# First modulation by quarters of columns, with the contraction of 1536 columns begun on each quarter's K-tiles

## The reference, cut to what matters

```
c_act = silu(c)                                    # c: 1 x 2048
mod   = c_act @ w_ada + b_ada                      # w_ada: 2048 x 12288
sh_m, sc_m, gt_m, sh_f, sc_f, gt_f = split(mod, 6)
h     = rmsnorm(x, pre_mix_norm) * (1 + sc_m) + sh_m
proj  = h @ w_in                                   # w_in: 2048 x 8208
o     = concat(hgrn2_group(proj[:, :4096]), gdn_group(proj[:, 4096:]))
```

## Time and profile before

| | us |
|---|---|
| median of three runs (range) | 3039.1 (3035.82 to 3039.58) |
| the profiled execution | 3033.75 |
| its span, first to last instruction | 3032.0 |
| TensorE / VectorE / ACT busy, share of the span | 89% / 61% / 41% |
| first matmul of the contraction | 146.06 |
| mean granted TensorE clock | 0.964 |

### The profile page before, as it was taken

The page is one execution under the profiler, slowest core; times in us unless marked ns, Lnnn a source line. Parts: engine busy times, 40 slices in busy tenths (PEclk is TensorE's granted clock), DMA queues, the critical chain, the costliest instruction groups (busy, mean ns, idle before and its releaser), DMA issues.

```text
span 3032.0 us, 32738 instructions
## 1 busy us (share of the span) xinstructions
PE 2685.3 (89%) x12601; PEld 2214.3 (73%) x12601; DVE 1855.7 (61%) x2095; ACT 1232.3 (41%) x1505; POOL 58.8 (2%) x92
## 2 busy tenths in 40 slices
PE   2299998576969999999997999998989999999985
PEld 1188886576858888888875877776768888888874
DVE  6878765866575555555575456567455565656454
ACT  0244445342444434444433444444544434344342
POOL 2000000000010000000000000000000000000000
PEclk9999999978989999999998999998999999999998
DMA  9677886014755555555573534443435555455451
GB/s 343 281 265 262 291 290 222 28 69 152 256 199 195 187 186 188 186 194 181 206 265 118 187 111 143 142 160 139 166 134 185 192 169 197 170 200 180 151 170 68
DMA packets 142026, 563.26 MB, mean 186 GB/s; under 512 B 9512, under 2 KB 13719, under 8 KB 133600
## 3 DMA queue, kind: packets, MB, share of 16 engines
q1 hardware_dynamic: 137216, 537.95, 51.1%
q0 software_dynamic: 4704, 23.86, 2.2%
HBM read 557.32 MB, written 4.46 MB: 185 GB/s over the span
## 4 chain that ended last, share of the span: by engine, by line
PE 72%; DVE 13%; issue 8%; ACT 4%; DMA 2%; POOL 1%; DVEq 0%; ACTq 0%; POOLq 0%
PE banks L386 22%; PE banks L388 22%; PE banks L387 22%; ACT weights_high L332 3%; DVE weights_low L343 2%; DMA raw_weights<-in_w_ada 2%; PE banks L444 2%; DVE mod_in L362 1%; DVE x_rows L429 1%; DVE modulation L2152 1%; DVE lhs_low L457 1%; POOL small L531 1%; DVE proj L810 1%; DVE proj L794 0%; DVE modulation L2150 0%
## 5 line engine op out<-in xcount | busy, mean ns | idle before, releaser
L343 DVE TENSOR_TENSOR weights_low<-raw_weights,weights_high 128x1024 fp32r<-128x1024 f32 (+2 forms) x862 | 1019.4, 1189 | 955.8 <-ACT weights_high L332 953.1
L332 ACT ACTIVATE weights_high<-raw_weights 128x1024 fp32r<-128x1024 f32 (+2 forms) x862 | 882.8, 1030 | 1127.2 <-PE banks L388 1073.1
L386 PE MATMUL banks<-weights_high,lhs_high 128*128 128x512 f32 (+1 forms) x2304 | 911.7, 396 | 33.0 <-DVE weights_low L343 15.6
L388 PE MATMUL banks<-weights_high,lhs_low 128*128 128x512 f32 (+1 forms) x2304 | 898.2, 390 | 0.0
L387 PE MATMUL banks<-weights_low,lhs_high 128*128 128x512 f32 (+1 forms) x2304 | 897.2, 389 | 0.0
L386 PEld LDWEIGHTS banks<-weights_high,lhs_high 128*128 128x128 f32 x2304 | 435.2, 189 | 124.7 <-DVE weights_low L343 14.2
L388 PEld LDWEIGHTS banks<-weights_high,lhs_low 128*128 128x128 f32 x2304 | 434.8, 189 | 89.8
L387 PEld LDWEIGHTS banks<-weights_low,lhs_high 128*128 128x128 f32 x2304 | 435.4, 189 | 83.9
L386 PE MATMUL banks<-weights_high,hid_high 128*128 128x512 f32 x856 | 337.4, 394 | 19.4 <-DVE hid_low L2129 9.8
L387 PE MATMUL banks<-weights_low,hid_high 128*128 128x512 f32 x856 | 335.4, 392 | 0.0
L388 PE MATMUL banks<-weights_high,hid_low 128*128 128x512 f32 x856 | 335.3, 392 | 0.0
(11 more groups left out here) (387 smaller groups left out, 2049.0 us busy)
## 6 DMA issues: line engine op xcount, KB each, us to landing
raw_weights<-in_w_ff SPq DMA_DIRECT2D x128, 1024.0 KB, 4.9
raw_weights<-in_w_in SPq DMA_DIRECT2D x112, 1024.0 KB, 5.4
raw_weights<-in_w_ada SPq DMA_DIRECT2D x96, 1024.0 KB, 5.1
raw_weights<-in_w_up SPq DMA_DIRECT2D x80, 1024.0 KB, 4.8
raw_weights<-in_w_down SPq DMA_DIRECT2D x42, 1024.0 KB, 5.1
raw_weights<-in_w_out SPq DMA_DIRECT2D x32, 1024.0 KB, 5.0
raw_weights<-in_w_ckv SPq DMA_DIRECT2D x8, 1024.0 KB, 5.0
raw_weights<-in_w_up SPq DMA_DIRECT2D x16, 384.0 KB, 3.3
```

The lines of the kernel that those rows point to most:

```text
L332: act.activation(WHI[:, u % SPN, 0:c.width], RAW[:, n % RAWN, k % 2, 0:c.width], ACT.Copy).then_inc(S("high_made"), 1)
L343: dve.tensor_tensor(WLO[:, u % SPN, 0:c.width], RAW[:, n % RAWN, k % 2, 0:c.width], WHI[:, u % SPN, 0:c.width].bitcast(F32), ALU.subtract) ...
L386: nc.tensor.matmul(o, x, hi, start=(k == 0), stop=False)
L388: mm = nc.tensor.matmul(o, y, hi, start=False, stop=(k == c.kn - 1))
```

## The change

The two parts of the first modulation are made in four quarters of 512 columns. A load of `w_ada` is now 512 rows x 512 columns (four K-tiles). Quarter 0 has eight loads; quarters 1 to 3 have after each pair of modulation loads one load of `w_in`, 128 rows x 1536 columns (chunk 4 and the first half of chunk 5), of the K-tiles of the quarter before; four such loads close the sequence. The scale part is summed by VectorE (16 operations of 512 columns a quarter). Of the shift part TensorE takes all K-tiles in quarter 0 and two of four in the others, with the column of `c_act` as its only stationary column; VectorE sums the rest. A row copy on ACT and single-column matmuls turn a quarter's sums into columns. x is scaled by its rstd, transposed while it is without modulation (`XTURN`), and ACT applies scale and shift per partition. Six banks hold the 1536 columns.

`w_in` goes on with the second half of chunk 5; the 32 modulation loads beside the chunks are now five each in chunks 6, 7, 0, 1 and six each in chunks 2 and 3. `c`, the tables and x are issued by ACT; POOL does the memset of `MOD`; the order of its small loads is new.

```diff
-        segs = [pair_in(4, 0, 1, 0, ("norm_in", "conv0")), pair_in(6, 0, 1, 1, ("conv1", "conv2")), pair_in(0, 2, 2, 2)]
+        for n, j in enumerate((6, 7, 0, 1, 2, 3)):
+            for x in ((1, 2, 3, 5, 7), (1, 2, 3, 5, 6, 7))[n >= 4]:
+                in_ada.setdefault(j, {})[x] = divmod(sum(len(y) for y in in_ada.values()), 8)
+        segs = [(1, [in1(5, "conv0", None, 512), in1(6, "conv1", in_ada[6]), in1(7, "conv2", in_ada[7])] +
+                 [in1(j, None, in_ada[j]) for j in range(4)])]
+        for q in range(4):
+            for j in range(4):
+                FIRST_LOADS += [("mod", q, 0, j), ("mod", q, 1, j)] + ([("w", 4 * q - 4 + j)] if q else [])
+        FIRST_LOADS += [("w", 12 + j) for j in range(4)]
+        def sp_first(sp):
+            for n, x in enumerate(FIRST_LOADS):
+                if n >= RAWN:
+                    y = FIRST_LOADS[n - RAWN]
+                    if y[0] == "w":
+                        sp.wait_ge(S("low_made"), 2 * y[1] + 2)
+                    else:
+                        sp.wait_ge(S("rows_summed"), PE_SUMS[y])
+                        if DVE_SUMS[y]:
+                            sp.wait_ge(S("mod_summing"), DVE_SUMS[y])
...
+            def shift_rows(q, j):
...
+                for kk in range(pe_rows(q)):          # 4 in quarter 0, else 2
+                    kt = 4 * j + kk
+                    mm = nc.tensor.matmul(PS[0:1, 6, :], COND[:, kt:kt + 1], raw[:, QC4 * kk:QC4 * kk + QC4],
+                                          start=(kt == 0), stop=(j == 3 and kk == pe_rows(q) - 1))
+            def mod_columns(q):
+                pe.wait_ge(S("mod_summing"), DVE_SUMS["mod", q, 1, 3])
+                pe.wait_ge(S("row_copied"), q + 1)
...
+            def k_tile(k):
+                pe.wait_ge(S("h_low"), k + 1)
+                unit(k, 0)                            # 12 matmuls, 1024 columns
+                unit(k, 1)                            # 6 matmuls, 512 columns
...
+            shift_rows(0, 0)
...
+            shift_rows(0, 1)
+            pe.wait_ge(S("x_scaled"), 2)
+            for r in range(8):                        # four transposes of x each, banks 4 and 5
...
+            shift_rows(0, 2)
...
+            for h in range(AH):                       # the twelve distance matmuls
...
+            shift_rows(0, 3)
+            mod_columns(0)
+            for q in range(1, 4):
+                for j in range(4):
+                    shift_rows(q, j)
+                    k_tile(4 * q - 4 + j)
+                mod_columns(q)
+            for k in range(12, 16):
+                k_tile(k)
...
+            def turned_input(q):                      # ACT
+                act.wait_ge(S("mod_made"), q + 1)
+                for k in range(4 * q, 4 * q + 4):
+                    last = act.activation(XTURN[:, k, :], XTURN[:, k, :], ACT.Identity, scale=SCALE_COL[:, k:k + 1],
+                                          bias=SHIFT_COL[:, k:k + 1])
...
+                for k in range(4 * q, 4 * q + 4):
+                    act.activation(LH[:, k, :], XTURN[:, k, :], ACT.Copy).then_inc(S("h_high"), 1)
...
+            shift_row(0)                              # ACT, after the twelve distance copies
+            turned_input(0)
+            for q in range(1, 4):
+                for j in range(4):
+                    high(4 * q - 4 + j)
+                shift_row(q)
+                turned_input(q)
...
+            for q in range(1, 4):                     # VectorE
+                for j in range(4):
+                    sums(("mod", q, 0, j))
+                    if j == 0:
+                        mod_cols(q - 1)
+                    sums(("mod", q, 1, j))
+                    if j == 0:
+                        input_low(q - 1)
+                    low(4 * q - 4 + j)
+            mod_cols(3)
+            input_low(3)
...
+                def first_turn(pe):                   # before the first conv transposes
+                    for b in range(4):
+                        pe.wait_ge(S(f"bank_free{b}"), 1)
+                    pe.wait_ge(S("rest_copied"), TT)
```

More of the change, by code:

```diff
@@ L53, in ada_after, with number @@
     def ada_after(self, j):
-        return self.mid * (j == 1) if self.mid else int(bool(self.ada) and j % 2 == 1)
+        return self.mid * (j == 1) if self.mid else int(bool(self.ada) and j in self.ada)
     def load_of(self, j):
         return self.at["n"] + j + sum(self.ada_after(x) for x in range(j))
[L63 to L67, removed]
+def number(segments, first_loads, first_out):
+    u, n, done, signals = 2 * KT, len(first_loads), [1] * 4, [1, 1, 1, 0]
+    rel = {m: ("lo", 2 * x[1] + 2) for m, x in enumerate(first_loads) if x[0] == "w"}
+    prev = dict(end=dict(u=u - 1, done=list(done), banks=4, width=UW, out=first_out, col=first_out[2]))
+    ada = 0
     for iters, chunks in segments:
@@ L205, in whole, with in1 @@
             return chunks
-        def pair_in(base, step, iters, half_row, phases=(None, None)):
-            return (iters, [ck("w_in", 0, (base + j) * UW, KT, UW, first, ("copy", P, (base + j) * UW, step * UW),
-                               col_step=step * UW, ada=(half_row, 1, 4 * j), phase=phases[j]) for j in range(2)])
+        def in1(j, phase=None, ada=None, col0=0):
+            return ck("w_in", 0, j * UW + col0, KT, UW - col0, first, ("copy", P, j * UW + col0, 0), phase=phase, ada=ada)
         def up1(c, step=0, phase=None, ada=None):
@@ L306, in sp_chunk @@
                         continue
[L307 to L320, removed]
+                    half_row, q = c.ada[k // 2]
+                    x0 = 2 * D + half_row * UW
+                    load(RAW[:, n % RAWN, :, :], a["w_ada"][q * 256:q * 256 + 256, x0:x0 + UW].rearrange(
+                        "(j p) n -> p j n", p=128))
         def unit_dma(c, k):
@@ new lines, in block_pair @@
+        DVE_SUMS, PE_SUMS = {}, {}
+        for x in FIRST_LOADS:
+            if x[0] == "mod":
+                DVE_SUMS[x] = (max(DVE_SUMS.values()) if DVE_SUMS else 0) + (4 if x[2] else 4 - pe_rows(x[1]))
+                PE_SUMS[x] = (max(PE_SUMS.values()) if PE_SUMS else 0) + (0 if x[2] else 1)
+        COND = COLS[:, 112:128]
+        GAIN0, BIAS0, BIAS1 = COLS[:, 224:240], COLS[:, 352:368], COLS[:, 368:384]
+        SHIFT_COL, SCALE_COL = GATES[:, 1, :], GATES[:, 0, :]
+        COND_ROWS = LLF[0:16, 13, 0:128]
@@ L635, in pe_norm_in @@
[L635 to L651 removed]
+                act.activation(TOE[:, h % 4, :], PS[:, 2 + h % 4, 0:384], ACT.Copy).then_inc(S("distance_row"), 1)
@@ new lines, in dve_first @@
+            link(dve.tensor_scalar(SM[:, 168:176], l0, 1.0, None, ALU.subtract))
+            for q in range(1, 4):
[9 more added lines that the diff above has]
+            input_low(3)
+            for k in range(12, 16):
+                low(k)
@@ L675, in straight, with act_first_rest @@
+            dve.wait_ge(S("bias_in"), 16)
+        def act_first_rest(act):
+            act.wait_ge(S("unit_used"), 2 * KT)
+            for t in range(TT):
+                act.activation(P[:, t, 5 * UW:5 * UW + 512], PS[:, 4 + t, :], ACT.Copy).then_inc(S("rest_copied"), 1)
         def straight(program):
```

361 lines of the change are left out of this document (229 added, 132 removed).

## The result

| | kernel before | changed kernel |
|---|---|---|
| median, us (range) | 3038.39 (3032.22 to 3041.72), 6 runs | 3047.99 (3045.22 to 3051.53), 6 runs |
| ratio, 95% interval | | 1.0035 [1.0022, 1.0048] |
| profiled execution / span | 3033.75 / 3032.0 | 3045.22 / 3043.1 |
| first contraction matmul | 146.06 | 76.65 |
| 1536 columns through | about 211 | 217.7 |

A forecast was written before the change was run, and what follows sets the result against it. TensorE, busy 89%, was taken as the bound, leaving the first 146 us to gain. First contraction 81, 1536 columns at 215 us (211 before), plus 299: end of w_in 514 against 506.4, +8, so 3047 us; range 3015 to 3080.

The forecast's parts named there:

- distances: Twelve distance matmuls on TensorE before quarter 0's last four shift matmuls: 15.5 us, through at 63.5 us.
- single-column matmuls at a border: At each quarter's end TensorE does 24 single-column passes that turn sums into columns: 2.9 us.
- last four K-tiles: After the last border: four K-tiles at TensorE's pace, 16.3 us, and about 3 us for starting cold.
- Loads and the start: Up to the first contraction: fourth load there at 30 us, first contraction at 81 us, 65 us earlier than now.
- The K-tile pace: Within quarters: the chain gives 15.3 us for two K-tiles; written out with the queue's order, 8.1 us each.
- Buffers as the cause: Within quarters: a shift load's buffer is given back only after its shift matmuls, behind the previous K-tile's contraction; four buffers.
- Borders: At each quarter's end: 14 us in place of 8.1, VectorE waiting about 5 us for TensorE; last border 13.5.
- The other 6656 columns: Contraction after the first 1536 columns: 294 us plus join, convolution and extra modulation loads, 299 us in sum.
- Rival 1: Quarters: loads set the pace, buffers free in time; end of w_in at 467, -40 us, some 2999; chance 0.10.
- Rival 3: Nothing to be seen: start at 76 and K-tile 7.9 take 7 us off the sum, 3040; chance 0.23.
- Rival 2: Half clock in the K-tiles: 11.3 us each, TensorE-bound, +38 us, 3085; chance 0.08.
- The unseen price: One-column matmul, in no profile row: taken as two passes, between one pass (0.43 us) and two cold ones (1.7).

The follow-up runs named there:

- keeping the clock: Changed kernel plus one-column matmuls with unused results (three, two before a quarter's first, third K-tile; four before the last four): 3042.05 us, 1.0023 of the kernel before.
- the rows ahead: Changed kernel, but within a quarter TensorE does the next K-tile's two shift matmuls before this one's contraction: 3036.95 us, 1.0009 of the kernel before.
- VectorE relieved: Changed kernel, but TensorE does all four shift matmuls of every load in quarters 1 to 3, VectorE no shift sums: 3045.22 us, 1.0039 of the kernel before.

## Why the prediction was right, and where it was off

The time came within 1 us of the forecast (its kernel before within 1 us too), and the mechanism is the one forecast: the early start is used up by a K-tile pace twice TensorE's and by three borders. That the number fits to 1 us is in part luck: the start was 4.4 us too late in the sum and the quarters and borders 8 us too short, the end of `w_in` came 5 us later than forecast, and behind it the difference shrank by 3. By its steps (the forecasts of single chunks are the shares of its sum of 299):

| step | forecast | measured |
|---|---|---|
| fourth load; x scaled; transposes | 30; 38; 44.5 | 30.23; 38.09; 44.26 |
| distances | 48 to 63.5 | 47.78 to 62.1 |
| last four shift matmuls | 6.8 | 5.0 |
| columns | 3.4 | 2.5 |
| first contraction | 81 | 76.65 |
| one K-tile within a quarter | 8.1 | 8.7 |
| single-column matmuls at a border | 2.9 | 4.2, 4.3, 3.4 |
| border | 14, 14, 13.5 | 14.9, 14.9, 14.0 |
| last four K-tiles | 19.3 | 18.7 |
| end of the 1536 columns | 215 | 217.7 |
| half chunk 5, chunk 6, chunk 7 | 28, 51, 45.8 | 28.4, 50.4, 47.1 |
| chunks 0 to 3 | 174 | 173.8 |
| end of `w_in` | 514 (+8) | 519 (+12.7) |

- **Loads and the start** (right in order, forecast 4.4 us too late). The fourth load landed to the quarter us. The two terms taken too long are the last shift matmuls and the columns, both taken at half clock: the clock rose during the shift matmuls. That error hid part of the next.
- **The K-tile pace** (the term that was mis-sized). The cycle was forecast as contraction 4.1, shift matmuls 1.7, landing 5, sums 3.3, low part 1.2, 15.3 for two; its rows are 6.9, 1.82, 5.32, 3.1, 1.27, together 18.45 (76.65 to 95.10). Only the contraction is off, by 2.8 us, and it runs at half clock: K-tile 0 begins with matmuls 0.43 us apart and comes to 0.23 only at its 13th of 18. In every quarter the first and the third K-tile are slow (6.2 to 6.3 and 5.4 us from first to last weight load), the second and the fourth, which follow a K-tile and its shift matmuls at once or nearly, are not (3.8). Before the third TensorE had stood 3.4 to 3.8 us, before K-tile 0 4.5; at the first two borders it stood 2.8, but there the clock had fallen before, in the column matmuls. My sentence "at the other borders a slower first K-tile lies beside VectorE's sums" failed: the sums can't start before the load, and the load not before the contraction and the shift matmuls behind it, so a slower K-tile lies in front of them. Three quarters (26.2 us from first to fourth K-tile against 24.3) and the borders are 8 us over the forecast together; keeping the clock gave back 5.3, or 8.7 with the later start taken off, of which 6 lie here and 2.7 in the last four K-tiles, where the forecast had charged 3.
- **Buffers as the cause** (right): the chain shows the load going out 0.02 us behind the shift matmuls, and with the rows ahead the quarters are 3.5 to 4.9 us shorter, with VectorE relieved they are not. How much of that gain is the order alone isn't shown, since the clock rose with it.
- **Borders** (right in kind, one term too small): VectorE stood 7.3 us a time in L797 (21.8 in three) for TensorE's column matmuls; I had said 5, and the border is 0.9 longer. The term is the 24 single-column passes: at the 0.213 us that the same sum takes for the sixteen before, they would be 5.1 us and not the 2.9 put down, for which the prediction names no row; they took 4.2 and 4.3 at the first two borders, where the clock fell among them, and 3.4 at the last. What follows them, scaling x to the low part, was some 0.5 us shorter than forecast.
- **The other 6656 columns** (right to 2 us): 301.4 against 299; chunk 7 was 1.3 longer, and 1.7 is the time from the first to the last of the final four bank copies, which the sum didn't have.
- **From 519 us to the end** the difference fell from 12.7 to 11.1 in the profiled spans and 9.6 in the medians. What gives the rest back is open; it is less than what two executions differ by.

Rival 1 (the loads set the pace) is refuted for this kernel by the DMA share of 0.53 to 0.82 between 24 and 212 us, and a part of it came next: with the rows ahead 30 us run at 377 GB/s. Rival 3 had the start at 76, and that came, but its K-tile of 7.9 did not. Rival 2 (half clock in the K-tiles) was partly true: every second K-tile runs for the most part at half clock, and the fillers gave back 6 us of that before the last four K-tiles, where the rival had 38. The Trainium skill, TensorE: Matmul & The Clock Gate, section "HAM oscillation — how this bites in real kernels", was cited for it: where a K-tile's work is shorter than the wait behind it, each starts cold. The trace agrees for half of them, and not to the letter: the third K-tiles begin at full clock and lose it behind three matmuls, the wait before them (3.4 to 3.8 us) is shorter than the work before it (about 6 us with the shift matmuls), and at two borders the clock fell without a wait. The unseen price, the one-column matmul, came as assumed: two passes, each 0.85 us at half clock and 0.43 at full.

## What to carry to other kernels

An early start is worth only what the pace behind it keeps: write out the cycle that gives one buffer back, from contraction to load to sum to contraction, and put in each term at the clock it will run at. When a consumer holds a scarce buffer, its small work goes ahead of the large one in its queue, and a gain at one queue must be followed through the next one's order before it is counted. Two edits that each take a term out of different chains need not add: after the first, ask again what the second stands behind.

## What the runs showed of the hardware

Matmuls with one stationary column and 512 moving ones raised the clock here. In the changed kernel's first group of eight passes of 512 columns the weight loads stand 0.85 us apart and then 0.43 (columns: start, us; idle before):

```profile
10.23 0.11 PEld L636 LDWEIGHTS banks<-raw_weights,columns 128*1 128x1 f32 x2 [3.40 <-issue]
11.06 0.13 PEld L636 LDWEIGHTS banks<-raw_weights,columns 128*1 128x1 f32 x1 [0.72 <-issue]
...
13.62 0.13 PEld L636 LDWEIGHTS banks<-raw_weights,columns 128*1 128x1 f32 x1 [0.73 <-issue]
14.13 0.09 PEld L636 LDWEIGHTS banks<-raw_weights,columns 128*1 128x1 f32 x1 [0.38 <-issue]
14.56 0.08 PEld L636 LDWEIGHTS banks<-raw_weights,columns 128*1 128x1 f32 x1 [0.34 <-issue]
```

TensorE had stood 3.4 us before them. Matmuls with 128 stationary columns and one moving stayed at half clock for all of the earlier trace rows, and the 33-row distance matmuls stayed there in the earlier trace rows; such single-column matmuls even lost the full clock at two borders here. Behind shift matmuls at full clock, the same distance matmuls here began fast (their weight loads 0.182 to 0.333 us, median 0.234) and fell back. That makes a one-column matmul a usable filler, where enough of them stand in the gap: with three before a quarter's first K-tile and four before the last four the time gained more than they took, with two before a third K-tile nothing was gained (5.4 us as before).
